# Mixer outputs re-read and transposed on VectorE in the next down phase, and part of a residual row moved to ScalarE and GpSimd

## What is computed

```python
def swiglu(x, w_gate, w_up, w_down):
    return (jax.nn.silu(x @ w_gate) * (x @ w_up)) @ w_down

def trunk_layer(x, ...):
    x = layer_norm(ALPHA * x + 0.5 * swiglu(x, f1_wg, f1_wu, f1_wd), ln_f1_g, ln_f1_b)    # x1
    m, new_a, new_b = token_mixers(x, ...)    # input projection, width-31 and width-3 causal
                                              # convolutions, layer norm, output projection
    x = layer_norm(ALPHA * x + m, ln_mix_g, ln_mix_b)                                     # x2
    x = layer_norm(ALPHA * x + 0.5 * swiglu(x, f2_wg, f2_wu, f2_wd), ln_f2_g, ln_f2_b)    # y
```

## Time and profile before

| | |
|---|---|
| time, median of 3 runs | 1190.62 us (1190.33 to 1191.14) |
| the profiled execution | 1190.56 us, of which the span of its slowest core (core 2) is 1189.0 us |
| spans of the 8 cores | 1186.7 to 1189.0 us |
| busy in the span | TensorE 1171.3, VectorE 613.1, ScalarE 236.9, GpSimd 189.9 us |
| granted TensorE clock | 0.998 to 0.999 on all cores |

### The profile page before, as it was taken

The page is one execution under the profiler, slowest core; times in us unless marked ns, Lnnn a source line. Parts: engine busy times, 40 slices in busy tenths (PEclk is TensorE's granted clock), DMA queues, the critical chain, the costliest instruction groups (busy, mean ns, idle before and its releaser), DMA issues.

```text
span 1189.0 us, 20095 instructions; the slowest of 8 cores (1186.7 to 1189.0 us)
## 1 busy us (share of the span) xinstructions
PE 1171.3 (99%) x7099; PEld 638.2 (54%) x7144; DVE 613.1 (52%) x930; ACT 236.9 (20%) x439; POOL 189.9 (16%) x302
## 2 busy tenths in 40 slices
PE   8999999999999999999999999999999999999997
PEld 4544444455555666554455555545444466666443
DVE  2223218866555464719876656473736522222366
ACT  3211110021222335410022122325310012112000
POOL 0111102311110132312211110122212210000111
PEclk9999999999999999999999999999999999999999
DMA  8899886987767479895477676579864254443033
GB/s 282 127 196 154 157 139 169 195 191 121 118 112 117 109 144 185 170 209 142 151 160 115 108 111 120 115 144 177 176 164 142 71 110 84 72 71 89 29 103 106
DMA packets 76850, 162.21 MB, mean 136 GB/s; under 512 B 8976, under 2 KB 34768, under 8 KB 75456
## 3 DMA queue, kind: packets, MB, share of 16 engines
q0 software_dynamic: 28352, 76.07, 41.9%
q1 hardware_dynamic: 48400, 84.86, 24.4%
...
## 4 chain that ended last, share of the span: by engine, by line
PE 92%; DMA 4%; DVE 2%; issue 1%; ACT 0%; SPq 0%; POOL 0%; DVEq 0%; POOLq 0%; ACTq 0%
PE ps L581 48%; PE ps L645 25%; PE ps L745 11%; PE ps L1028 4%; DMA sb_xr<-x1s 3%; PE ps L863 1%; DMA sb_RW<-xta 1%; PE ps L663 1%; DVE sb_RW L807 1%; PE ps L434 1%; PE ps L969 0%; PE ps L997 0%; PE ps L651 0%; DVE sb_xr L493 0%; DVE sb_xr L490 0%
## 5 line engine op out<-in xcount | busy, mean ns | idle before, releaser
L581 PE MATMUL ps<-sb_xB,sb_ring 128*128 128x352 bf16 (+1 forms) x2112 | 319.5, 310 | 0.0
L581 PE MATMUL ps<-sb_xA,sb_ring 128*128 128x512 bf16 (+1 forms) x1472 | 311.6, 370 | 1.7 <-DVE sb_ring L1204 0.9
L588 DVE TENSOR_TENSOR sb_hT<-sb_sg,ps 128x352 bf16<-128x352 f32 (+3 forms) x224 | 129.5, 579 | 346.7 <-PE ps L581 319.6
L645 PE MATMUL ps<-sb_RW,sb_hT 128*128 128x512 bf16 x1333 | 293.1, 379 | 1.8 <-issue 0.3
L581 PEld LDWEIGHTS ps<-sb_xB,sb_ring 128*128 128x128 bf16 x2112 | 205.9, 98 | 106.9 <-issue 1.1
L586 ACT ACTIVATE sb_sg<-ps 128x352 f32<-128x352 f32 (+3 forms) x224 | 113.6, 508 | 585.5 <-PE ps L581 464.7
L581 PEld LDWEIGHTS ps<-sb_xA,sb_ring 128*128 128x128 bf16 x1472 | 142.9, 98 | 156.9 <-issue 4.2
L645 PEld LDWEIGHTS ps<-sb_RW,sb_hT 128*128 128x128 bf16 x1364 | 133.2, 98 | 160.1 <-issue 0.4
L372 POOL DMA_DIRECT2D sb_ring<-wgu x84 | 46.5, 554 | 459.7 <-PE ps L581 398.4
L482 POOL TENSOR_SCALAR sb_mv<-sb_mv 128x1 f32<-128x1 f32 (+1 forms) x50 | 44.5, 890 | 355.4 <-DVE sb_mv L480 348.3
L474 DVE SCALAR_TENSOR_TENSOR sb_xr<-sb_xr,ps 128x1024 f32<-128x1024 f32 x47 | 57.3, 1219 | 84.2 <-PE ps L645 66.6
...
## 6 DMA issues: line engine op xcount, KB each, us to landing
sb_ring<-wgu POOLq DMA_DIRECT2D x84, 512.0 KB, 6.7
sb_RW<-wd POOLq DMA_DIRECT2D x33, 512.0 KB, 9.6
...
sb_RW<-uscr SPq DMA_DIRECT2D x128, 67.0 KB, 4.9
sb_xr<-xp SPq DMA_DIRECT2D x16, 512.0 KB, 6.6
x1s<-sb_xr SPq DMA_DIRECT2D x16, 512.0 KB, 3.8
sb_xr<-x1s SPq DMA_DIRECT2D x16, 512.0 KB, 9.1
x2s<-sb_xr SPq DMA_DIRECT2D x16, 512.0 KB, 6.9
```

Of the source, the lines that this page charges most:

```text
L581: ins = e.matmul(bank(bk, n), lhsT=ring[:, s, c:c + 128], rhs=xcol(k, tok0, n), start=(k == 0), stop=(k == KC - 1))
L588: P.op("dve", lambda e: e.tensor_tensor(out=hT[:, f, l0:l0 + n], in0=sg[:, q, :n], in1=bank(bu, n), op=ALU.mult), reads=[("sg", q)] + pst( ...
L645: ins = e.matmul(ps[:n, (yb + h) * 512:(yb + h + 1) * 512], lhsT=hT[:, f, l0:l0 + n], rhs=wd[:, f, h * 512:(h + 1) * 512], start=(f == 0), ...
```

## The change

The mixer's `cast_xb` and `xpose` of the 16 prompt tiles are taken out. Instead a new helper `again(b)` re-reads each x2 row of block b from HBM into a new two-slot bf16 buffer `xb2` (POOL DMA with cast, after the store of that row) and passes it to `xmove`. For block 0 the loads of tiles 0 and 1 are issued where the mixer of block 0 refills its weight window, ahead of those four weight loads; tiles 0 and 1 are moved when the matmuls of the first tile of `down(0, 1)` are recorded, and tiles 2 to 7 join the list `queued` at tiles 8, 9, 10, 12, 13 and 14 of that phase. Each move then issues the reload of the tile two further on. For block 1 the same is done in `down(1, 0)`: tiles 8 to 11 at its first tile, tiles 12 to 15 at its tiles 2 to 5. The list `queued` is now also emptied in `ln_tail`. Besides, for tiles 8 to 13 and 16 of `down(0, 1)` the row of L510 is computed by a scaled copy on ScalarE and an addition of `lnp` on GpSimd.

```diff
+        xb2 = sb("xb2", [128, 2, D], BF16)
...
-        def xmove(t, c):
+        def xmove(t, c, buf=None, key="xb"):
             s, d = tqr(), xsr()
+            src = xb if buf is None else buf
             P.op("dve", lambda e: e.transpose(out=tq[:, s, :].rearrange("p (q h k l) -> p k q h l", q=4, h=2, k=KC),
-                                              in_=xb[:, c, :].rearrange("p (k q h l) -> p k q h l", q=4, h=2, k=KC)),
-                 reads=[("xb", c)], writes=[("tq", s)])
+                                              in_=src[:, c, :].rearrange("p (k q h l) -> p k q h l", q=4, h=2, k=KC)),
+                 reads=[(key, c)], writes=[("tq", s)])
...
+        queued = []
+
+        def flush():
+            while queued:
+                queued.pop(0)()
+
         def ln_tail(ctx):
...
+            flush()
...
-        def ln_tail2(ctx):
+        def ln_tail2(ctx, off=False):
...
-            while queued:
-                xmove(*queued.pop(0))
+            flush()
...
-            P.op("dve", lambda e: e.scalar_tensor_tensor(
-                out=xr[:n, s, :], in0=xr[:n, s, :], scalar=mv[:n, m, 2:3], in1=lnp[:n, :],
-                op0=ALU.mult, op1=ALU.add), reads=[("xr", s), ("rs", m), "lnp"], writes=[("xr", s)])
+            if off:
+                P.op("act", lambda e: e.activation(out=xr[:n, s, :], in_=xr[:n, s, :], func=AF.Identity, scale=mv[:n, m, 2:3]),
+                     reads=[("xr", s), ("rs", m)], writes=[("xr", s)])
+                P.op("pool", lambda e: e.tensor_tensor(out=xr[:n, s, :], in0=xr[:n, s, :], in1=lnp[:n, :], op=ALU.add),
+                     reads=[("xr", s), "lnp"], writes=[("xr", s)])
+            else:
+                P.op("dve", lambda e: e.scalar_tensor_tensor(
+                    out=xr[:n, s, :], in0=xr[:n, s, :], scalar=mv[:n, m, 2:3], in1=lnp[:n, :],
+                    op0=ALU.mult, op1=ALU.add), reads=[("xr", s), ("rs", m), "lnp"], writes=[("xr", s)])
...
-                        c = ln_tail2(ctx)
+                        c = ln_tail2(ctx, b == 1 and i < len(tl) - 2)
...
-                                queued.append((t, c))
+                                queued.append(lambda: xmove(t, c))
...
-                for k in at(i, 5, True):
-                    xpose(tl[k], xbs[k], ((3, 3, 3, 7), (3, 6, 3, 7))[par][k])
-                for k in at(i, 4, True):
-                    xbs[k] = cast_xb(tl[k], xslot[k])
...
+        def again(b):
+            def load(j):
+                t = 8 * b + j
+                P.op("pool", lambda e: e.dma_start(out=xb2[:, j % 2, :], in_=spill(1, t)),
+                     reads=[("x2", t)], writes=[("xb2", j % 2)], dma="xb2_%d" % (j % 2))
+
+            def move(j):
+                xmove(8 * b + j, j % 2, xb2, "xb2")
+                if j + 2 < 8:
+                    load(j + 2)
+            return load, move
...
                     wstate["lim"] = 40
+                    load(0)
+                    load(1)
                     for _ in range(NWIN):
                         fetch_win()
...
+        load, move = again(0)
         merge(up_items(0, 1), mixer(0, 0, pend, 3.0, 1.0, 1.0))
         load_ln(0)
-        pend = down(0, 1, 2.0 * ALPHA, 4.0 * EPS, False, npar=2)
+        aux = {i: [lambda j=j: queued.append(lambda: move(j))] for i, j in ((0, 2), (1, 3), (2, 4), (5, 5), (6, 6), (7, 7))}
+        aux[0] = [lambda: [move(0), move(1)]] + aux[0]
+        pend = down(0, 1, 2.0 * ALPHA, 4.0 * EPS, False, npar=2, aux=aux)
         merge(up_items(1, 0), mixer(1, 1, pend, 2.0, 0.65, 0.7))
+        load, move = again(1)
+        load(0)
+        load(1)
         left[0]()
         load_ln(2)
-        (_, tail) = down(1, 0, 2.0 * ALPHA, 4.0 * EPS, True, npar=2, aux={2: [lambda: left[1]()]})
+        aux = {i: [lambda i=i: queued.append(lambda: move(i + 2))] for i in range(2, 6)}
+        aux[0] = [lambda: [move(j) for j in range(4)]]
+        aux[2].append(lambda: left[1]())
+        (_, tail) = down(1, 0, 2.0 * ALPHA, 4.0 * EPS, True, npar=2, aux=aux)
```

More of the change, by code:

```diff
@@ L495, in ln_tail @@
                 op0=ALU.mult, op1=ALU.add), reads=[("xr", s), ("rs", m), ("lnb", 1)], writes=[("xr", s)])
-        queued = []
-        def ln_tail2(ctx):
+        def ln_tail2(ctx, off=False):
             (t, n, s, m) = ctx
```

## The result

The changed kernel takes 1206.7 us (median of three runs, 1206.4 to 1207.3) against 1190.6 before: a ratio of 1.0135 (95% interval 1.0121 to 1.0149), 16.1 us slower. The profiled execution took 1206.4 us, 15.8 more than that of before. The forecast was 1193.6, with a range up to 1200.

The account below looks back on a forecast made before the run. TensorE, busy 1171.3 of 1189.0 us, was taken as the bound. From 1190.56 us, 7.2 of removed transposes came off and 10.2 of delay behind the border was added: 1193.6 us, range 1187 to 1200.

Parts of the forecast that it names:

- Removal: Mixer: 16 transposes of 0.45 us leave TensorE, all of it on the path, saving 7.2 us.
- Cost on VectorE: `down(0, 1)`: the second transpose is paid for by the row that leaves; the GpSimd addition takes 2.3 us.
- Rival (1): `down(0, 1)`: the GpSimd addition holds VectorE too, 0.7 us per tile on five tiles, 3.5 us more: 1197.1 us; 25%.
- Reload 2: `down(0, 1)`, tile 8: tile 2's reload lands behind the weights at 543.0 (541.6 to 546); VectorE waits some 6 us.
- Tile 12: `down(0, 1)`: TensorE waits 5.6 us for a bank, until ScalarE's copy of tile 16's product ends at 562.5.
- just in time: `down(0, 1)`: L474 of tile 9 comes at 545.4, its banks being wanted at 547.48.
- The border: Behind `down(0, 1)`: the second up item waits for tile 7's placement at 608.9; TensorE 10.2 us late, tile 12's 5.6 included.
- The clock: TensorE: a pause that the clock answers would make the forecast wrong; no size given.
- Rival (2): `down(0, 1)`: tile 2's reload is in time, tile 7's placement 4.3 us late: 1187.7 us, 1191.1 with Rival (1); 25%.
- Rival (3): Behind `down(0, 1)`: only the least cost, 1.3 us, with VectorE up with TensorE at tile 14: 1184.7 us; 8%.

Follow-up runs that it names:

- no67: The changed kernel with tiles 6 and 7 of block 0 left to TensorE (`xpose`) instead of moved; 1199.0 us.
- noadd: The changed kernel with the GpSimd addition left out and the ScalarE pass kept; 1206.3 us.
- early: The changed kernel with block 0's reloads 0 and 1 issued in the mixer and their moves made ahead of the weight refill; 1205.0 us.
- xb3: The changed kernel with a third place for a reload, an idle slot of `xb`, so tile 2's reload is issued ahead of the weights; 1202.7 us.
- row10: The changed kernel with tile 10's spill row back on VectorE, so nothing stands ahead of tile 16's copy on ScalarE; 1205.9 us, one run.
- early2: The changed kernel with first reloads and moves far earlier in the mixer, so reloads, scratch writes and row loads are issued ahead of the weights; 1200.3 us.

## Why the prediction was wrong

The direction and the places were right: a VectorE wait on `xb2` ahead of tile 8's L507, a TensorE wait at tile 12 released by ScalarE's copy, one at the second up item released by tile 7's placement, and `down(1, 0)` at nothing. The sum failed by size, 13 us, most of it in one step: the delay behind the border was forecast at 10.2 us and came to 17.9 and, by the clock, 1.7 more, because the forecast priced the late reload alone and put VectorE's hold, the slots of `tq` and the clock at nothing. By its steps, in the chain of the profiled execution:

- **Removal, 7.2 us.** Measured 1.4 in mixer 0 and 3.6 in mixer 1. The step failed for block 0: "all of it on the path" is true of the transposes, but they also covered a wait. Without them TensorE waits in mixer 0 for ScalarE's row (L1009 on L999), 0 to 1.9 us by core, and 0.5 us or more on every core for VectorE at an up item; in before there is only the first of these, 0.5 and 0.8 us on two cores. In no67, with two transposes left, nothing at all is gained there: the same wait, and 0.8 us for a cast. Mis-sized by 2.2 us. For block 1 the step held.
- **Cost on VectorE.** The addition takes 2.34 us (2.3 forecast). Rival (1) is the case: L509 takes 1.94 us beside it instead of 1.28, so 0.66 on each of tiles 9, 10, 12, 13 and 14 by the time of tile 7's transpose: 3.3 us, for the 3.5 that the rival had. The forecast put it at nothing. The Trainium skill, "SBUF — State Buffer", section "Who interferes with whom", states that a VectorE instruction with two SBUF inputs contends with a GpSimd one that reads SBUF, and the trace agrees with it in this direction too. As noadd shows, taking the hold away did not shorten the slowest core.
- **Reload 2.** Transposed at 545.58, forecast 543.0, bounds 541.6 to 546: inside, 2.6 us late. (The upper bound was added up wrongly: four weights, the chunk and the reload at 3.05 us per 256 KB behind 528.7 give 550, not 546.) Reload 1 was late already: its transpose started at 531.62, for a landing forecast at 528.7; from there to the transpose of reload 2 it took 14.0 us, for 14.3. That this was the deciding step failed: early and xb3 removed the wait, and a row load or a scratch write took its place. The prediction counted the moves' own writes as 1.4 us of extra pace, and not as something to be waited for; they landed 7.8 to 13.6 us after issue, which frees the first slot of `tq` only 1.4 us ahead of the late transpose.
- **Tile 12.** 7.97 us for 5.6, and tile 11 2.07 for "just in time". Tile 11's wait follows from the 2.6 us. The copy of tile 16 ended at 566.75 for 562.5, by the 2.6, two holds (1.3) and 0.43 us for a slot of `tq`; TensorE came 1.9 us later too.
- **The border.** The second up item started 17.9 us later than in the earlier trace rows, for 10.2. From the reload 2.6, from the five holds 3.3, from a wait for a slot of `tq` (599.11) that no step had 1.7; the 0.1 that is left is the balance of smaller differences (0.43 more at a slot of `tq`, 0.9 more on SP ahead of the gather, 1.3 less from the gather to its use).
- **The clock.** Named as what could make it wrong, and not priced. It took 1.7 us at the border (5.30 us for 3.62). What it took behind tile 12 does not add to this, since the placement that the border waits for does not depend on TensorE there.
- **The cores.** The slowest lost 1.1 us more than the median (15.8 against 14.7); the stage's length varies between the cores by 2.3 us in after and 0.2 in before, and in `down(1, 0)` the slowest core alone waits 1.4 us. No step had it.

Together 2.2 + 2.6 + 3.3 + 1.7 + 0.1 + 1.7 + 1.1 = 12.7, and with the 3.0 forecast 15.7 of the 15.8 between the profiled executions. This says where the time lies in one chain, not what taking a term away would give: xb3, noadd and row10 got back 4 us or less. Rival (2) failed with the forecast: with the reload in time neither its 1187.7 nor, with (1) on top, its 1191.1 was to be had. Nearest to its condition is early2, whose second up item is 9.7 us late for the 7.8 that (2) and (1) have together (4.3 and 3.5); the slow item and the mixer's missing gain, which neither rival had, come on top. Rival (3)'s condition, VectorE up with TensorE at tile 14, was met in no67 alone of the runs that move block 0's tiles, and TensorE itself was late by then.

The range was too narrow at the top for the same reason: it was built of one chain with its terms at their ends, and left out that a wait taken from the chain is met again at the next transfer.

What stays open: which of bytes and number of transfers makes the crowd; whether block 0's moves could lie in mixer 0 (tried for two tiles only); what early2's order with tiles 6 and 7 by `xpose` would take; and the size of row10's gain, which rests on one run.
